# Gate products in plain fp32 and sixteen more tokens taken row by row, in a two-block kernel on one Trainium2 core

## The reference

```
q = (xb @ wq).reshape(PEER_BLOCK, PEER_HEADS, 2, PEER_HALF)
s = einsum('thpd,hpkd->thpk', q, sub_keys)
s_top, i_top = lax.top_k(s, PEER_TOPK)
...                                             # 16 x 16 candidates per head, the best 16
g = softmax(best_s)
act = gelu(einsum('thkd,td->thk', expert_u[experts], xb))
return einsum('thk,thkd->td', g * act, expert_v[experts])
```

## Time and profile before

| | |
|---|---|
| median of 3 runs | 2395.98 us (2395.8 to 2396.16) |
| the profiled execution | 2396.43 us, of which 2394.6 us span from first to last instruction |
| mean granted TensorE clock | 0.998 of full speed |
| gate steps | about 679 to 966 us of the span |
| last U tiles | 966 to 1077.7 us |
| V stage | 1077.7 to about 1590 us |

### The profile page before, as it was taken

The page is one execution under the profiler, slowest core; times in us unless marked ns, Lnnn a source line. Parts: engine busy times, 40 slices in busy tenths (PEclk is TensorE's granted clock), DMA queues, the critical chain, the costliest instruction groups (busy, mean ns, idle before and its releaser), DMA issues.

```text
span 2394.6 us, 35817 instructions
## 1 busy us (share of the span) xinstructions
PE 2359.3 (99%) x12844; PEld 2121.6 (89%) x12844; DVE 1564.1 (65%) x2831; ACT 944.2 (39%) x1487; POOL 1244.7 (52%) x705
## 2 busy tenths in 40 slices
PE   7999999999999999999999999999999999999998
PEld 4878888899999999999999999998778888888886
DVE  5258435689999999779999999892366125322201
ACT  4374333344455555333333333342354223222312
POOL 2305443447899999455555554444304444444443
PEclk9999999999999999999999999999999999999999
DMA  7237522337978998999999999943203222322231
GB/s 285 80 115 253 191 88 97 132 107 273 321 247 300 313 329 309 393 388 415 413 416 413 417 417 404 366 161 114 75 20 100 97 97 88 97 96 96 95 99 71
DMA packets 179613, 526.14 MB, mean 220 GB/s; under 512 B 18240, under 2 KB 70896, under 8 KB 178224
## 3 DMA queue, kind: packets, MB, share of 16 engines
q1 hardware_dynamic: 120928, 345.24, 40.2%
q0 software_dynamic: 43024, 159.14, 17.2%
q10 hardware_dynamic: 15552, 20.36, 2.4%
HBM read 474.93 MB, written 49.73 MB: 219 GB/s over the span
## 4 chain that ended last, share of the span: by engine, by line
PE 93%; POOL 3%; DVE 1%; ACT 1%; DMA 0%; issue 0%; SPq 0%; ACTq 0%; DVEq 0%
PE bank L1388 22%; PE bank L1390 22%; PE bank L1389 22%; PE pair L1389 6%; PE pair L1388 6%; PE pair L1390 6%; POOL wlo L716 2%; PE pair L1743 1%; POOL T L796 1%; PE bank L1911 1%; PE pair L1529 1%; PE bank L1568 1%; PE bank L1555 1%; POOL X L782 1%; PE pair L1684 1%; PE bank L1894 0%
## 5 line engine op out<-in xcount | busy, mean ns | idle before, releaser
L716 POOL TENSOR_TENSOR wlo<-wraw,whi 128x1024 fp32r<-128x1024 f32 x303 | 739.9, 2445 | 745.6 <-ACT whi L863 744.3
L863 ACT ACTIVATE whi<-wraw 128x1024 fp32r<-128x1024 f32 x456 | 481.9, 1058 | 661.4 <-PE pair L1390 369.8
L1388 PE MATMUL bank<-HH,whi 128*128 128x512 f32 (+1 forms) x2048 | 738.9, 361 | 3.4 <-DVE HL L2133 1.9
L1390 PE MATMUL bank<-HH,wlo 128*128 128x512 f32 (+1 forms) x2048 | 735.2, 359 | 0.0
L1389 PE MATMUL bank<-HL,whi 128*128 128x512 f32 (+1 forms) x2048 | 735.2, 359 | 0.0
L1388 PEld LDWEIGHTS bank<-HH,whi 128*128 128x128 f32 x2048 | 384.5, 188 | 46.5 <-issue 5.3
L1390 PEld LDWEIGHTS bank<-HH,wlo 128*128 128x128 f32 x2048 | 384.3, 188 | 40.1
L1389 PEld LDWEIGHTS bank<-HL,whi 128*128 128x128 f32 x2048 | 384.6, 188 | 39.6 <-issue 0.5
L789 POOL DMA_INDIRECT VROW<-in_w,which x128 | 205.9, 1608 | 192.1 <-DVE YROW L2544 179.9
L2476 DVE TENSOR_TENSOR wlo<-wraw,whi 128x1024 fp32r<-128x1024 f32 x153 | 186.3, 1218 | 23.2 <-ACT whi L863 20.5
L782 POOL DMA_INDIRECT X<-in_u_rows,which x128 | 147.2, 1150 | 58.2 <-DVE dots L2318 33.1
(11 more groups left out here) (444 smaller groups left out, 3798.8 us busy)
## 6 DMA issues: line engine op xcount, KB each, us to landing
wraw<-in_w SPq DMA_DIRECT2D x456, 512.0 KB
gate_dram<-GS SPq DMA_DIRECT2D x24, 1024.0 KB
GJ<-gate_dram SPq DMA_DIRECT2D x32, 768.0 KB
act_dram<-actb ACTq DMA_DIRECT2D x108, 184.0 KB
AJ<-act_dram SPq DMA_DIRECT2D x108, 184.0 KB
adaw<-in_ada SPq DMA_DIRECT2D x32, 512.0 KB
ada<-in_ada SPq DMA_DIRECT2D x16, 512.0 KB, 14.7
NB<-in_nab POOLq DMA_DIRECT2D x4, 1024.0 KB
```

What stands on the lines that cost most here:

```text
L716: nc.gpsimd.tensor_tensor(wlo[:, slot, :, :].rearrange("p k c -> p (k c)"), wraw[:, slot, :, :].rearrange("p k c -> p (k c)"), whi[:, slot ...
L863: nc.scalar.activation(whi[:, slot, :, :].rearrange("p k c -> p (k c)"), wraw[:, slot, :, :].rearrange("p k c -> p (k c)"), ACT.Copy).then ...
L1388: pe.matmul(out_, ah, bh, start=first, stop=False, **kw)
L1390: return pe.matmul(out_, al, bh, start=False, stop=last, **kw)
```

## The change

- `FT` becomes 32: 16 more tokens go by rows. `SD` becomes 352, `STEPS` 88, `DOTS` 160 (row fetches, dots and row additions alike).
- The gate products are no longer split. `OI` and `OG` are plain fp32, `OG` has 512 elements per partition, the four products of a step have 128 columns each, and ScalarE alone copies all out (`gate_out`). `gate_high` and `gate_sum` are gone.
- 92 dots stand at the 88 gate steps, 32 (the few tokens') in the last U tiles, 8 in the V stage.
- Of U tiles 43 to 102, the low halves of the odd ones are made by VectorE at the end of a step. GpSimd then waits for VectorE (`w_low_vector`), writes one element (`low_mark`) and raises `w_lo` itself, so that `w_lo` still counts up in order.
- Row fetches in the gate steps follow the number of dots instead of every second step.

```
-FT = 16
+FT = 32
...
-GATE_DOT = 2
-PSUM_DOTS = TOP_DOTS + STEPS // GATE_DOT
-U_DOTS = 112
+GATE_DOTS = 92
+PSUM_DOTS = TOP_DOTS + GATE_DOTS
+TAIL_DOTS = 32
+U_DOTS = PSUM_DOTS + TAIL_DOTS
...
-V_DOT_TILES = [10 * m // 3 + 1 for m in range(32)][:DOTS - U_DOTS]
+V_DOT_TILES = [8 * m + 1 for m in range(DOTS - U_DOTS)]
...
-        OI = a2("OI", [P, 8, P], FR)
-        OG = a2("OG", [P, 2, 2, 4, P], FR)
+        OI = a2("OI", [P, 8, P])
+        OG = a2("OG", [P, 2, 4, P])
...
+        def low_step(t):
+            return (t - 4 * GATE_IT - 3) * STEPS // GATE_TILES + 1
+        def by_vector(t):
+            return t % 2 == 1
+        def gate_dots(q):
+            return GATE_DOTS * q // STEPS
...
+            def vector_low():                                  # GpSimd
+                passed[0] += 1
+                pool.wait_ge(w_low_vector, passed[0])
+                nc.gpsimd.memset(low_mark, 0.0).then_inc(w_lo, 1)
             for q in range(STEPS):
                 offsets_j(q)
-                if (lows - gate0 - 3) * STEPS // GATE_TILES + 1 == q:
-                    lo(G0["U"] + lows, lows % R)
+                if low_step(lows) == q:
+                    if by_vector(lows):
+                        vector_low()
+                    else:
+                        lo(G0["U"] + lows, lows % R)
                     lows += 1
-                if q >= 2 * GATE_DOT and q % GATE_DOT == 0:
+                while fetched < R + TOP_DOTS + gate_dots(max(q - 2, 0)):
                     fetch_u(fetched)
                     fetched += 1
...
+            def gate_out(q):                                   # ScalarE
+                act.wait_ge(g_done, q + 1)
+                if q % 16 == 0 and q >= 32:
+                    act.wait_ge(g_out[q // 16 % 2], 64 * (q // 32))
+                t = 4 * (q % 16)
+                nc.scalar.activation(GS[:, q // 16 % 2, :, t:t + 4], bank[4 + q % 3].rearrange("p (t j) -> p j t", t=4), ACT.Copy)\
+                    .then_inc(g_evac, 1)
...
             def gate_group(q):                                 # TensorE
                 pe.wait_ge(og_ready, q + 1)
...
+                if q >= 3:
+                    pe.wait_ge(g_evac, q - 2)
+                for e in range(4):
+                    mm = pe.matmul(bank[4 + q % 3][:, e * P:(e + 1) * P], OI[:, 4 * (q % 2) + e, :], OG[:, q % 2, e, :],
+                                   start=True, stop=True)
+                mm.then_inc(g_done, 1)
...
             for q in range(STEPS):                             # VectorE
                 if q % 32 == 0:
                     window(q // 32)
                 indices_hot(q)
-                if q >= 2:
-                    gate_sum(2 * q - 4)
-                    gate_sum(2 * q - 3)
                 gates_hot(q)
-                if q % GATE_DOT == GATE_DOT - 1:
+                while dotted[0] < TOP_DOTS + gate_dots(q + 1):
                     dot()
+                while low[0] < U_POOL and low_step(low[0]) <= q + 1:
+                    if by_vector(low[0]):
+                        lo(G0["U"] + low[0], low[0] % R, w_low_vector)
+                    low[0] += 1
```

More of the change, by code:

```diff
@@ L72 @@
 TAIL = P - 4 * GATE_IT - GATE_TILES
-U_POOL = 4 * GATE_IT + GATE_TILES + 3
+U_TAIL = 4 * GATE_IT + GATE_TILES + 3
+U_POOL = 103
 FETCH_AT = 13
@@ L148, in build @@
         rr = sb("rr", [P, 2, S])
+        low_mark = st[:, 23:24]
         rms, rstd = rr[:, 0, :], rr[:, 1, :]
@@ L221, in build @@
         gsel = a1("gsel", [P, TB, P])
-        GHT = a1("GHT", [P, SD], FR)
-        GLT = a1("GLT", [P, SD], FR)
+        GT = a1("GT", [P, SD])
         which = a1("which", [P, 2, P], U32)
@@ L353, in build @@
         w_lo = sem("w_lo")
+        w_low_vector = sem("w_low_vector")
         tile_done = sem("tile_done")
@@ L636, in store_g @@
             def store_g(b, part):
-                sp.wait_ge(g_evac, min(b * 32 + 32, 2 * STEPS))
+                sp.wait_ge(g_evac, min(b * 16 + 16, STEPS))
                 sp.dma_start(gate_dram[8 * part:8 * part + 8, :, b, :].rearrange("g i c -> i g c"),
@@ L822, in _ @@
             for t in range(lows, U_POOL):
-                lo(G0["U"] + t, t % R)
-            for k in range(fetched, U_DOTS + R):
+                if by_vector(t):
+                    vector_low()
+                else:
+                    lo(G0["U"] + t, t % R)
+                while fetched < R + PSUM_DOTS + (t - U_TAIL + 1) * TAIL_DOTS // (P - U_TAIL):
+                    fetch_u(fetched)
+                    fetched += 1
+            u_fetches = min(U_DOTS + R, DOTS)
+            for k in range(fetched, u_fetches):
                 fetch_u(k)
@@ L827, in _ @@
                 pool.wait_ge(g_out[b], 64 * TD)
-            fetched = U_DOTS + R
+            fetched = u_fetches
             for n, k in enumerate(V_ROWS):
@@ L1102, in _ @@
                 act_tile(m, u, 16 * (m // 2))
[L1104 to L1111, removed]
+            def gate_out(q):
[5 more added lines that the diff above has]
+                    .then_inc(g_evac, 1)
             def gate_tile(u):
@@ L1119, in _ @@
             for n in range(STEPS + 2):
-                for h in range(2 * n - 4, 2 * n - 2):
-                    if h >= 0:
-                        gate_high(h, 64 * (h // 64) if h % 32 == 0 and h >= 64 else None)
+                if n >= 2:
+                    gate_out(n - 2)
                 for u in range(units(n) // 8, units(n + 1) // 8):
@@ L1773, in v_tile @@
                 add_up(u, WH[:, u, :], WL[:, u, :], first, last, **kw)
-            pe.wait_ge(g_evac, 2 * STEPS)
+            pe.wait_ge(g_evac, STEPS)
             v_tile(0, 0, first=True, order=(2, 3, 4, 5, 6, 7, 0, 1), freed=G0["V"] - 1)
@@ L2419, in _ @@
             nc.vector.tensor_copy(ITS[:, 0:SD], bank[4][:, 0:SD])
-            then(nc.vector.tensor_copy(GHT[:, :], bank[6][:, 0:SD]))
-            nc.vector.tensor_tensor(GLT[:, :], bank[6][:, 0:SD], GHT[:, :].bitcast(F32), ALU.subtract).then_inc(gt_split, 1)
+            nc.vector.tensor_copy(GT[:, :], bank[6][:, 0:SD]).then_inc(gt_split, 1)
             v.wait_ge(gt_split, 1)
@@ L2429, in window @@
                 nc.vector.tensor_copy(gate_window[:, 0:m], ITS[:, i * P:i * P + m])
[L2430 to L2433, removed]
+                then(nc.vector.tensor_copy(gate_window[:, P:P + m], GT[:, i * P:i * P + m]))
             def indices_hot(q):
                 if q >= 2:
-                    v.wait_ge(g_done, 2 * q - 2)
+                    v.wait_ge(g_done, q - 1)
                 n, ring = q % 32, slice(4 * (q % 2), 4 * (q % 2) + 4)
@@ L2446, in gates_hot, with lo @@
                 v.wait_ge(oj_ready, q + 1)
-                oj = OJ[:, q % 4, :, :].rearrange("p t j -> p (t j)")
-                nc.vector.scalar_tensor_tensor(OG[:, q % 2, :, :, :].rearrange("p w t j -> p w (t j)"), bc(oj, 1, 2), 0.0,
-                                               bc(gate_window[:, P + 8 * n:P + 8 * n + 8], 2, P), ALU.is_equal, ALU.mult)\
+                nc.vector.scalar_tensor_tensor(OG[:, q % 2, :, :], OJ[:, q % 4, :, :], 0.0,
+                                               bc(gate_window[:, P + 4 * n:P + 4 * n + 4], 2, P), ALU.is_equal, ALU.mult)\
                     .then_inc(og_ready, 1)
[L2452 to L2458, removed]
+            def lo(g, slot, done=w_lo):
+                v.wait_ge(w_hi, g + 1)
+                nc.vector.tensor_tensor(wlo[:, slot, :, :].rearrange("p k c -> p (k c)"),
+                                        wraw[:, slot, :, :].rearrange("p k c -> p (k c)"),
+                                        whi[:, slot, :, :].rearrange("p k c -> p (k c)").bitcast(F32),
+                                        ALU.subtract).then_inc(done, 1)
+            low = [4 * GATE_IT + 3]
             for q in range(STEPS):
@@ L2488, in expert_weights @@
                 v.wait_ge(w_known, i + 1)
+            v.wait_ge(g_done, STEPS)
             then(nc.vector.memset(kept0[:, :, SD:TD * P], 0.0))
[L2491 to L2495, removed]
+            for t in range(U_TAIL, P):
+                if t == U_POOL:
+                    v.wait_ge(w_lo, G0["U"] + U_POOL)
+                if t >= U_POOL:
+                    lo(G0["U"] + t, t % R)
+                while dotted[0] < PSUM_DOTS + (t - U_TAIL + 1) * TAIL_DOTS // (P - U_TAIL):
                     dot()
```

2 lines of the change are left out of this document (1 added, 1 removed).

## The result

The changed kernel takes 2461.9 us (median of 4 runs, 2458.9 to 2465.18), the kernel before 2396.07 us (4 runs, 2395.8 to 2396.28): a ratio of 1.0275, 95% interval 1.0263 to 1.0287. It is slower by 65.8 us; 2461 was forecast. The profiled execution took 2465.18 us, its span is 2463.4 us against 2394.6 before.

The account below looks back on a forecast made before the run. TensorE (busy 99%) was taken as the bound, with thin margins to VectorE, GpSimd and transfers. 2396.4 - 10.8 (U) + 94 (gate steps) - 14.3 (V) = 2465, set to 2461 us for overlap; range 2410 to 2500.

Parts of the forecast that it names:

- The loop: Gate steps: GpSimd's fetch stands behind its wait for VectorE's low half and one step ahead of its dot; +94 us.
- first kind: Three-step round in the gate steps, GpSimd's own low half after the second fetch: l + 5.1 us, 12 rounds.
- second kind: Three-step round in gate steps 24 to 42 and 68 to 86, GpSimd's low half before the second fetch: l + 7.3.
- the lead lost: Rounds in the gate steps where two dots share a step, so the third fetch is needed at once: l + 9.5.
- The mark: Gate steps: from VectorE's low half through GpSimd's one-element write to the fetch issue, 0.38 us, the write 0.15.
- The landing, l: Gate steps: time from a fetch's issue until its row lands; 5.7 us, 7.8 during stores, mean 6.4, bounds 4.65 and 8.0.
- TensorE's pace: Gate steps: plain fp32 gate group 0.89 us instead of 0.48; 3.51 us a step with its blocks if nothing held it.
- Clash of low halves (rival): Gate steps: VectorE's low halves contend with GpSimd's for SBUF, up to 1.3 us each of 30, 2499 us; chance 0.07.
- Columns: U and V products: sixteen columns fewer save 6.6 ns per matmul, -40.6 us over both, -20.3 of it in V.
- V's transfers, +6: V stage: 1.67 MB a tile at 415 GB/s takes 4.01 us against TensorE's 3.84; +6 us, from 0 to 12.
- Last U tiles: Among the 68 U tiles outside the gate steps, where cheaper columns were to give -10.8 us in all.
- rival of hidden fetches: Gate steps go at TensorE's pace because row fetches are hidden: 2389 us, faster than before; chance 0.15.

Follow-up runs that it names:

- kernel 7: Changed kernel with GpSimd's row fetches both ahead of its low half or wait for VectorE's, and one step earlier: 2389.36 us, ratio 0.9971.
- kernels 2: Changed kernel with every row fetch one step earlier, two ahead of its dot, still behind the wait for VectorE's low half: 2400.87 us, ratio 1.002.
- kernel 6: Kernel before with only the gate products changed to plain fp32, copied out by ScalarE; 368 columns, 16 tokens by rows: 2425.61 us, ratio 1.0124.

## Why the prediction was right

The mechanism held, and so did the size of its term, the gate steps. Of the smaller terms several were off and cancelled: by stages, forecast and measured in us, U tiles ahead of the gate steps -6.3 and -2.4, gate steps +94 and +91.3, last U tiles -4.4 and +2.9, V -14.3 and -19.2, behind V nothing and -3.8. That the total (2461 for 2461.9) is right to 1 us is luck.

- **The loop.** Shown. It stands in the trace as it was written: mark, fetch, landing, dots, low half. Undoing one of its two conditions gives back 51 us (the fetch behind the wait) or 61 us (the lead of one step), undoing both 73; a pause inside it costs 22 us, and the same pause outside it nothing.
- **The sum over the rounds.** From the mark of step 3 to that of step 86 the trace has 28 rounds, 366.5 us in all. The 12 of the first kind take 11.5 us on average (l + 5.1 with l = 6.4: 11.5), the 12 of the second kind 13.8 (13.7), the 4 with the lead lost 15.6 (15.9). So each kind came out as priced. The recorded sum has a slip: 4 x 9.5 is 38 and not 36, which makes 366 and not 364. What lies outside the rounds is 11.7 us and not 17, and so the stage is 3 us shorter than forecast. Its lower bound was added up wrongly too: with l = 4.65 the three kinds give 126 + 143 + 57 = 326 us and not 337, so +56 and not +67.
- **The share of TensorE.** Forecast was that it waits 20% of the stage. The waits are 52.2 us, 14%; all that the stage takes beyond TensorE's own 304.1 us is 74 us, 20%. Up to 15 us of the difference go to a slower clock (last section).
- **The mark.** 0.38 us were allowed from low half to fetch; from about 782.1 to 782.41 it is some 0.3. The write itself, without a row then, takes 0.10 us and not 0.15.
- **The landing, l.** Called the weakest number. Outside the stores 5.7 us were put; 5.44 and 5.52 were measured in the round shown, and with l = 5.5 the formula for the second kind, l + 7.3, gives 12.8 for its 12.74. Beside the stores of `gate_dram` 7.8 were put; the longest in each of those rounds is 7.4 to 8.8. One of 8.52 (a fetch, a store, the dot of the fetched row):

```profile
808.69 0.95 POOL L796 DMA_INDIRECT X<-in_u_rows,which  x1
...
808.94 0.43 SPq L653 DMA_DIRECT2D gate_dram<-GS  x1
...
817.21 1.22 DVE L2347 CUSTOM_DVE_ANT_0 X<-X,bank 128x1024 f32<-128x1024 f32 x1 [5.29 <-DMA X<-in_u_rows,which]
```

- **TensorE's pace.** A plain fp32 group was priced at 0.89 us, and another price was named as a sign of being wrong. In kernel 7, undisturbed, the distance from the group to the next U product is 0.81 us, but the product behind that one follows after 0.25 us, where U products otherwise stand 0.16 apart:

```profile
700.43 1.05 PE L1772 MATMUL pair<-OG,OI 128*128 128x128 f32 x8
701.24 0.41 PE L1419 MATMUL bank<-HH,whi 128*128 128x352 f32 x1
701.49 0.32 PE L1420 MATMUL bank<-HL,whi 128*128 128x352 f32 x1
```

  So the group costs TensorE 1.06 - 0.16 = 0.90 us: the price was right.
- **Clash of low halves (rival).** Refuted. VectorE's 29 low halves in the gate steps take 1.22 to 1.30 us, those in the round shown among them, not up to 1.3 us more, as the rival had it after the 2.48 of the earlier trace rows: each time GpSimd stands at its wait for them. "SBUF — State Buffer", "Who interferes with whom", of the Trainium skill speaks of two operations that overlap in time. The trace does not contradict it: here only one engine is at work.
- **Columns.** -6.6 ns a product was right: in V TensorE's own work should fall by 20.3 us, and V became 19.2 shorter.
- **V's transfers, +6.** The term of the sum that was mis-sized: about 1 us. The count of rows a tile was too high. GpSimd's issues of the middle of V, grouped by line, are 105 in 300 us or 77.5 tiles, 1.36 a tile and not 1.46, since only 4 of the 8 dots in V still need a fetch there:

```profile
L803 POOL DMA_INDIRECT VROW<-in_w,which x79 | 144.7, 1831 | 114.7 <-DVE YROW L2561 113.8 <-issue 0.9
L803 POOL DMA_INDIRECT VROW<-in_w,few x25 | 32.2, 1287 | 8.6 <-issue 7.3 <-DVE T L2561 1.3
L796 POOL DMA_INDIRECT X<-in_u_rows,which x1 | 1.3, 1267 | 0.3 <-issue 0.3
```

  A tile then moves 1.61 MB, at 415 GB/s 3.89 us against TensorE's 3.84: 0.05 us over 60 tiles, 3 us, less what the buffers hold. The queues are as full as before (share 1.03, 413 GB/s); no fortieth of a span on any page of the profiles here shows more than 418 GB/s, so the 435 of the Trainium skill ("DMA: Bandwidth & Descriptors", "Bandwidth") stayed untested.
- **Last U tiles, 28 of the 68 outside the gate steps, 28 x 24 x 6.6 ns = -4.4.** Wrong in sign: +2.9. What was not foreseen: a tile of weights comes late. ScalarE's `whi` of the stage waits 28.8 us for weights, once 9.16 us, and TensorE stops for 3.57, after which its granted clock is 0.53 for 3.6 us (1086.0 to 1089.6):

```profile
1083.92 1.06 ACT L895 ACTIVATE whi<-wraw 128x1024 fp32r<-128x1024 f32 x1 [9.16 <-DMA wraw<-in_w]
...
1085.47 0.40 PE L1419 MATMUL bank<-HH,whi 128*128 128x352 f32 x1 [3.57 <-ACT actb L1105]
```

  SyncE had just issued the last parts of `gate_dram`, and stood 10.77 us at the next loads of weights:

```profile
1068.17 2.52 SPq L653 DMA_DIRECT2D gate_dram<-GS  x1
1070.73 10.77 SPq L569 DMA_DIRECT2D wraw<-in_w  x2
```

  That the stores are the cause is argued from this order, not tried. In kernel 7 the stretch from the last gate product to V is 112.5 us (983.3 to 1095.8), with smaller stalls; the -4.4 do not come there either.
- **First 40 U tiles, -6.3.** Only 2.4 us came: the gate steps begin at 676.4 instead of 678.8. Ahead of them TensorE now waits 2.9 us for VectorE's `gsel`, where before, with the dearer columns, it came later and did not wait; from 666.3 to 669.7 its granted clock is then 0.50, which takes some 1.7 us more. The start is not a firm number: kernels 2 and 7 have the same instructions up to there and begin the gate steps at 676.0 and 679.2.

```profile
665.15 0.33 PE L1760 MATMUL pair<-ident,gsel 128*128 128x128 f32 x1 [2.92 <-DVE gsel L2444]
```

- **The end.** A gain of 3.7 us that was not forecast lies behind ScalarE's last instruction, here with the span 2394.6 before and 2463.4 after:

```profile
2387.08 0.72 ACT L1365 ACTIVATE T<-X,fin 128x512 f32<-128x512 f32 x1 [0.29 <-POOL X L850]
```

```profile
2459.62 0.72 ACT L1396 ACTIVATE T<-X,fin 128x512 f32<-128x512 f32 x1 [0.29 <-POOL X L882]
```

  7.5 us remain after its start before, 3.8 after. From V's last product to the end of the span are 797.0 us in the changed kernel and 796.9 in kernel 7, but 800.8 before and in kernel 6, which also has 16 tokens by rows. The cause stays open.

The account of the spans: -2.4 + 91.3 + 2.9 - 19.2 - 3.8 (all behind V's last product) = +68.8. The rival of hidden fetches was given 2389 us; kernel 7, where they no longer hold TensorE, takes 2389.4. Its gate steps came as that rival has them (+17.2 us against the kernel before, where 34.1 - 7 for the stalls - 9.5 for the columns of 60 tiles is +17.6). The rest is luck: V gave 5 us and the end 4 more than was counted, the U tiles outside the gate steps some 12 less.

## What to carry to other kernels

When work is moved so that engine A waits for B, look at what stands behind the wait on A's queue: if it is a transfer that B needs a step later, its whole landing time joins each round, though no engine is busy. Issue the transfer ahead of the wait, or a step earlier; here both together turned +65.8 us into -6.6. And judge an edit that trades one engine's time for another's (experiment 6) only together with the one that spends what it frees.

## What the runs showed of the hardware that was not expected

In the changed kernel TensorE's granted clock falls to half nine times in the gate steps, each time in or behind a wait of 2.1 to 6.0 us, for 3.4 us mostly, so that such a wait costs more than its length. Not every wait has it: two of 2.65 and 2.18 us (up to 835.08 and 1046.69) had none. Around the wait of 2.11 us at 796 (windows, then TensorE in order of time):

```profile
793.00:796.00 3.00, 0.98 (x7) 0.69 (x5) 3.00 (x6) 0.00 (x0) 0.95 (x2) 1.00 0.18 57
796.00:799.40 3.40, 3.31 (x13) 3.31 (x14) 2.37 (x5) 0.60 (x1) 3.38 (x3) 0.50 0.85 293
799.40:803.00 3.60, 3.60 (x26) 3.60 (x26) 2.31 (x6) 1.92 (x3) 3.26 (x5) 1.00 0.68 205
```

```profile
796.09 2.08 PE L1772 MATMUL pair<-OG,OI 128*128 128x128 f32 x8 [2.11 <-DVE OG L2472]
```

For 3.4 us the clock is 0.50, 1.2 GHz, and the group, shown as 1.05 in kernel 7, takes 2.08. The mean over the gate steps is 0.96, where it was 1.00 before: by estimate 8% of the stage, 30 us, at half speed, which takes TensorE up to 15 us of full speed (two of the falls begin inside their waits). The prediction left that out, and its 28 rounds still took what it had priced: in the traced round VectorE, the fetches and GpSimd set the pace, and TensorE had 52 us to spare over the stage. That such a fall counts in full where TensorE is the pace was not tried. Kernel 7, without gaps, shows 1.00 over the stage.
